# Routing of a two-layer convolution and mixture-of-experts decoder step: the order of the mixer's tail, bf16 one-hot products for the ids, and the place of the first x gather

## The reference

```
h = layer_norm(ALPHA * h + m, ln1_g[i], ln1_b[i])          # m = mixer output
f = hierarchical_moe(h, ...)                               # below
h = layer_norm(ALPHA * h + f, ln2_g[i], ln2_b[i])

def hierarchical_moe(h, ...):
    glog = x @ rg_w + rg_b ; gprob = softmax(glog) ; gp, gidx = top_k(gprob, 1)      # 4 groups
    elog = (x @ re_w + re_b).reshape(-1, 4, 8) ; sel = the chosen group's 8 logits
    ew, eidx = top_k(softmax(sel), 2) ; ew = ew / ew.sum(-1)
    out = sum over the 2 experts: gate * (silu(x @ w_gate) * (x @ w_up)) @ w_down   # 32 experts, width 256
```

## Time and profile before

| | |
|---|---|
| median of 3 runs | 1351.43 us (1350.01 to 1351.71) |
| profiled execution, device time | 1347.05 us |
| its span in the profile | 1345.2 us |
| PE busy | 1036.2 us (77%) |
| DVE busy | 698.4 us (52%) |
| ACT busy | 323.8 us (24%) |
| POOL busy | 288.0 us (21%) |
| DMA | 277.49 MB, mean 206 GB/s |
| mean granted PE clock | 0.889 of full speed |

### The profile page before, as it was taken

The page is one execution under the profiler, slowest core; times in us unless marked ns, Lnnn a source line. Parts: engine busy times, 40 slices in busy tenths (PEclk is TensorE's granted clock), DMA queues, the critical chain, the costliest instruction groups (busy, mean ns, idle before and its releaser), DMA issues.

```text
span 1345.2 us, 16536 instructions
## 1 busy us (share of the span) xinstructions
PE 1036.2 (77%) x5223; PEld 636.4 (47%) x5223; DVE 698.4 (52%) x1286; ACT 323.8 (24%) x428; POOL 288.0 (21%) x399
## 2 busy tenths in 40 slices
PE   5999999947877788832869999359947887899940
PEld 4999984533322223311868998234443322233310
DVE  2323133363444444548399999943363444456438
ACT  2222120004333333412310110050004333344310
POOL 3333320001211111103327646000001211122200
PEclk8999999967998889975889999679967989899975
DMA  9251120085999999950130111000085999998933
GB/s 308 58 153 63 63 96 16 32 346 221 404 419 401 402 404 406 397 195 14 48 125 1 64 43 52 0 12 16 31 338 222 419 403 392 405 348 314 384 118 119
DMA packets 71739, 277.49 MB, mean 206 GB/s; under 512 B 14699, under 2 KB 33183, under 8 KB 45919
## 3 DMA queue, kind: packets, MB, share of 16 engines
q1 hardware_dynamic: 56248, 235.16, 44.9%
q10 hardware_dynamic: 4823, 22.09, 4.5%
q0 software_dynamic: 10624, 19.65, 3.9%
HBM read 268.66 MB, written 27.26 MB: 220 GB/s over the span
## 4 chain that ended last, share of the span: by engine, by line
PE 39%; DMA 24%; DVE 24%; SPq 5%; issue 5%; ACT 2%; POOL 0%; DVEq 0%; ACTq 0%; POOLq 0%; PEldq 0%
DMA ring<-in_moe_w_down_dram 21%; DVE ring L1511 14%; PE ps L890 13%; PE ps L910 10%; PE ps L988 7%; PE ps L1003 2%; SPq L421 2%; DMA ring<-in_sc_w_in_dram 1%; PE ps L922 1%; DVE bn L1192 1%; DVE h L1202 1%; DVE h L1415 1%; PE ps L974 1%; DVE h L1417 1%; SPq L414 1%
## 5 line engine op out<-in xcount | busy, mean ns | idle before, releaser
L988 PE MATMUL ps<-arena 128*64 128x512 f32 x1152 | 280.8, 644 | 62.5 <-DVE arena L1375 60.3
L988 PEld LDWEIGHTS ps<-arena 128*64 128x64 f32 x1152 | 87.4, 148 | 252.6 <-issue 159.3
L1511 DVE SCALAR_TENSOR_TENSOR ring<-arena,cvec,ring 128x528 f32<-128x528 f32 x360 | 189.6, 603 | 0.0
L890 PE MATMUL ps<-hT_hi,w_hi 128*128 128x296 f32 x640 | 145.5, 309 | 33.2 <-POOL w_lo L793 12.5
L1374 DVE COPY arena<-ring 128x1024 f32 x144 | 98.9, 687 | 132.2 <-SPq L487 105.6
L793 POOL TENSOR_TENSOR w_lo<-ring,w_hi 128x512 fp32r<-128x512 f32 x80 | 108.9, 1364 | 204.5 <-ACT w_hi L544 204.5
L910 PE MATMUL ps<-ring 128*128 128x512 f32 (+1 forms) x320 | 141.5, 602 | 11.9 <-ACT ring L736 11.9
L1003 PE MATMUL ps<-arena 128*64 128x512 f32 x576 | 131.5, 598 | 21.2 <-DVE arena L1391 21.2
L890 PE MATMUL ps<-hT_hi,w_lo 128*128 128x296 f32 x640 | 141.2, 302 | 0.0
L890 PE MATMUL ps<-hT_lo,w_hi 128*128 128x296 f32 x640 | 141.2, 302 | 0.0
L890 PEld LDWEIGHTS ps<-hT_hi,w_hi 128*128 128x128 f32 x640 | 105.4, 193 | 40.8 <-issue 30.0
(11 more groups left out here) (206 smaller groups left out, 1077.9 us busy)
## 6 DMA issues: line engine op xcount, KB each, us to landing
ring<-in_moe_w_gate_dram SPq DMA_DIRECT2D x64, 1024.0 KB, 7.7
ring<-in_moe_w_up_dram SPq DMA_DIRECT2D x64, 1024.0 KB, 9.9
ring<-in_moe_w_down_dram SPq DMA_DIRECT2D x64, 1024.0 KB, 13.2
ring<-in_sc_w_in_dram SPq DMA_DIRECT2D x12, 1024.0 KB, 12.0
ring<-in_cf_w_pw_dram SPq DMA_DIRECT2D x4, 1536.0 KB, 14.4
ring<-y_rows_dram ACTq DMA_DIRECT2D x6, 1024.0 KB, 7.1
ring<-in_sc_w_out_dram SPq DMA_DIRECT2D x2, 2048.0 KB, 8.4
x_rows_dram<-h ACTq DMA_DIRECT2D x8, 512.0 KB, 2.6
```

The lines of the kernel that those rows point to most:

```text
L890: last = nc.tensor.matmul(ps[:, pair + a, 0:HALF], w[:, i % 2, kc, :], x[:, k, a * HALF:(a + 1) * HALF], start=(k == 0 and w is w_hi and x ...
L988: ins = nc.tensor.matmul(ps[own, B_GU, :], xT_e[:, k, own], w_gu[:, x, c, i * 2 * F:(i + 1) * 2 * F], start=(k == 0), stop=(k == C - 1))
L1511: ins = nc.vector.scalar_tensor_tensor(out=out, in0=src, scalar=cf_tap(k, j), in1=out, op0=ALU.mult, op1=ALU.add)
```

## The change

Four things change, in both layers, and one is added once.

1. **Order of the mixer's tail.** PE's turn of the loop becomes: first half of project(t), turn of tile t-1, second half of project(t), route(t-1). DVE takes each half's `bn_stats` right after it has added that half, copies the turned tile t-1 between the halves, and reads logits t-1 at the end of the turn. ACT writes tile t-1 to `x_dram` and copies its half of `xT` ahead of the root of tile t.
2. **Ids by bf16 one-hot products.** `r_low` and `r_high` are bf16. An id needs more bits than bf16 has, so it is cut once, ahead of the first tail (`cut_ids`, four small DVE instructions), into a high and a low part; PE makes twenty bf16 products instead of ten in fp32.
3. **Ids ahead of the table.** On DVE the making of `yidx` and `xidx` stands ahead of the count of duos.
4. **First x gather ahead of the table.** POOL's first gather waits for `x_stored` and `ids_ready` only; the wait for `tab_ready` and the register load come after it.

```diff
+        id_parts = sb("id_parts", [P, 2, 2 * NT])
...
-        r_low = work[:, 2048:2048 + 2 * NT * P].rearrange("p (i n) -> p i n", n=P)
-        r_high = work[:, 3584:3584 + 2 * NT * NDUO].rearrange("p (i n) -> p i n", n=NDUO)
+        r_low = nc.alloc_sbuf_tensor_at("r_low", [P, 2 * NT, P], BF16, offset=base + 4 * (ARENA - WORK + 2048))
+        r_high = nc.alloc_sbuf_tensor_at("r_high", [P, 2, 2 * NT, NDUO], BF16, offset=base + 4 * (ARENA - WORK + 2048 + NT * P))
...
 (ACT)
                 for t in range(NT + 1):
-                    if t < NT:
-                        deviation(i * NT + t)
                     if t >= 1:
-                        copy_hT((i + 1) * NT + t - 1)
                         act.wait_ge(ln_done, i * NT + t)
                         n = ROWS[t - 1]
                         act.dma_start(x_dram[(t - 1) * P:(t - 1) * P + n, :], h[0:n, t - 1, :]).then_inc(x_stored, 16)
+                        copy_hT((i + 1) * NT + t - 1)
+                    if t < NT:
+                        deviation(i * NT + t)
...
 (POOL)
-                pool.wait_ge(tab_ready, l + 1)
-                last = last_duo(pool)
...
                 pool.wait_ge(x_stored, 16 * NT * (l + 1))
+                pool.wait_ge(ids_ready, l + 1)
                 load_x(0)
+                pool.wait_ge(tab_ready, l + 1)
+                last = last_duo(pool)
                 pool.wait_ge(x_turned[l], 1)
...
 (PE)
+                def turn(t):
+                    pe.wait_ge(ln_done, NT * 2 * layer + t + 1)
+                    turn_h(NT * (2 * layer + 1) + t)
+
+                for t in range(NT):
+                    if t >= 2:
+                        pe.wait_ge(z_done, 2 * NT * layer + 2 * (t - 1))
+                    project(layer, t, 0)
+                    if t >= 1:
+                        turn(t - 1)
+                    project(layer, t, 1)
                     if t == NT - 1:
                         pe.wait_ge(proj_done, 2 * NT * (layer + 1))
                         pe.sem_inc(mixer_slots_used, 2)
-                    if t >= 2:
-                        route(layer, t - 2)
                     if t >= 1:
-                        pe.wait_ge(ln_done, NT * 2 * layer + t)
-                        turn_h(NT * (2 * layer + 1) + t - 1)
+                        route(layer, t - 1)
+                turn(NT - 1)
                 route(layer, NT - 1)
...
-                    last = nc.tensor.matmul(ps[:, B_IDS, 0:NDUO], r_low[:, i, :], r_high[:, i, :],
-                                            start=(i == 0), stop=(i == 2 * NT - 1))
+                    for part in range(2):
+                        last = nc.tensor.matmul(ps[:, B_IDS, 0:NDUO], r_low[:, i, :], r_high[:, part, i, :],
+                                                start=(i == 0 and part == 0), stop=(i == 2 * NT - 1 and part == 1))
...
 (DVE, the loop of the tail)
+                        nc.vector.tensor_tensor(x, ps[0:n, 2 * (t % 2) + half, :], x, ALU.add).then_inc(z_done, 1)
+                        dve.wait_ge(z_done, i + 1)
+                        ins = nc.vector.bn_stats(bn[0:n, t, half, :], x)
+                        if half == 0 and t >= 1:
+                            turned(t - 1)
+                    step(ins)
+                    aggregate(m)
+                    ln_apply(m)
+                    if t >= 1:
+                        read_logits(layer, t - 1)
+                turned(NT - 1)
+                read_logits(layer, NT - 1)
...
+            def cut_ids():
+
+                dve.wait_ge(iota_made, 9)
+                whole, part = posi[:], posh[:, 0]
+                flat = ids[:].rearrange("p c t -> p (c t)")
+                step(nc.vector.tensor_copy(whole, flat))
+                step(nc.vector.tensor_scalar(part, whole, LOW_IDS, LOW_IDS, ALU.logical_shift_right, ALU.logical_shift_left))
+                step(nc.vector.tensor_copy(id_parts[:, 0], part))
+                step(nc.vector.tensor_tensor(id_parts[:, 1], flat, id_parts[:, 0], ALU.subtract))
...
-                step(tt(r_high, r_high, ids[:].rearrange("p c t -> p (c t)").unsqueeze(2).to_broadcast([P, 2 * NT, NDUO]),
-                        ALU.mult))
...
+                step(tt(r_high[:], r_here.unsqueeze(1).to_broadcast([P, 2, 2 * NT, NDUO]),
+                        id_parts[:].unsqueeze(3).to_broadcast([P, 2, 2 * NT, NDUO]), ALU.mult))
```

More of the change, by code:

```diff
@@ L898, in product_T, with project @@
                 pe.sem_inc(w_used, 1)
-            def project(layer, t):
+            def project(layer, t, half):
                 n = ROWS[t]
                 n0 = SEQ_MIX[layer] + MIX_SLOTS[layer] - 2
-                if t >= 2:
-                    pe.wait_ge(z_done, 2 * NT * layer + 2 * (t - 1))
-                for half in range(2):
-                    w = slot(n0 + half)[:, 0:C * DH].rearrange("p (j n) -> p j n", j=C)
-                    pe.wait_ge(weights_ready, n0 + half + 1)
-                    for j in range(C):
-                        last = nc.tensor.matmul(ps[0:n, 2 * (t % 2) + half, :], mixT[:, j, t * P:t * P + n],
-                                                w[:, j, :], start=(j == 0), stop=(j == C - 1))
-                    last.then_inc(proj_done, 1)
+                w = slot(n0 + half)[:, 0:C * DH].rearrange("p (j n) -> p j n", j=C)
+                pe.wait_ge(weights_ready, n0 + half + 1)
+                for j in range(C):
+                    last = nc.tensor.matmul(ps[0:n, 2 * (t % 2) + half, :], mixT[:, j, t * P:t * P + n],
+                                            w[:, j, :], start=(j == 0), stop=(j == C - 1))
+                last.then_inc(proj_done, 1)
             def route(layer, t):
@@ L926, in mixer_tail @@
             def mixer_tail(layer):
-                for t in range(NT + 1):
-                    if t < NT:
-                        project(layer, t)
+                def turn(t):
[8 more added lines that the diff above has]
+                    project(layer, t, 1)
                     if t == NT - 1:
@@ L1217, in mixer_tail, with turned @@
             def mixer_tail(layer):
-                for t in range(NT + 2):
-                    m = NT * 2 * layer + t
-                    if t < NT:
-                        n = ROWS[t]
-                        dve.wait_ge(h_scaled, NT * 2 * layer + t + 1)
-                        for half in range(2):
-                            i = 2 * NT * layer + 2 * t + half
-                            dve.wait_ge(proj_done, i + 1)
-                            x = h[0:n, t, half * DH:(half + 1) * DH]
-                            nc.vector.tensor_tensor(x, ps[0:n, 2 * (t % 2) + half, :], x, ALU.add).then_inc(z_done, 1)
-                        dve.wait_ge(z_done, 2 * NT * layer + 2 * t + 2)
-                        ln_stats(m)
-                        ln_apply(m)
-                    if t >= 2:
-                        read_logits(layer, t - 2)
-                    if 1 <= t <= NT:
-                        copy_hT(NT * (2 * layer + 1) + t - 1)
+                def turned(t):
+                    copy_hT(NT * (2 * layer + 1) + t)
@@ new lines, in mixer_tail @@
+                for t in range(NT):
+                    m, n = NT * 2 * layer + t, ROWS[t]
+                    dve.wait_ge(h_scaled, NT * 2 * layer + t + 1)
+                    for half in range(2):
+                        i = 2 * NT * layer + 2 * t + half
+                        dve.wait_ge(proj_done, i + 1)
+                        x = h[0:n, t, half * DH:(half + 1) * DH]
+                        nc.vector.tensor_tensor(x, ps[0:n, 2 * (t % 2) + half, :], x, ALU.add).then_inc(z_done, 1)
[4 more added lines that the diff above has]
+                    step(ins)
+                    aggregate(m)
+                    ln_apply(m)
+                    if t >= 1:
+                        read_logits(layer, t - 1)
@@ L1344, in route @@
                     dve.wait_ge(weights_ready, SEQ_MIX[layer] + 2)
+                dve.wait_ge(ids_turned, layer + 1)
+                found = ps[:, B_IDS, 0:NDUO]
+                step(nc.vector.tensor_scalar(idt[:], found, 0.5, blank[:, 0:1], ALU.is_lt, ALU.mult))
+                step(nc.vector.scalar_tensor_tensor(out=yidx[:], in0=found, scalar=-1.0, in1=idt[:], op0=ALU.add, op1=ALU.add))
+                nc.vector.tensor_scalar(xidx[:], yidx[:], 1, None, ALU.logical_shift_right).then_inc(ids_ready, 1)
                 tiles = incl[0:1, 0, E - 1:E]
@@ L1351, in route @@
                     nc.vector.tensor_scalar(tab[:, T_LAST + i:T_LAST + i + 1], duos, float(i + 1), None, ALU.subtract)
-                dve.wait_ge(ids_turned, layer + 1)
-                found = ps[:, B_IDS, 0:NDUO]
-                step(nc.vector.tensor_scalar(idt[:], found, 0.5, blank[:, 0:1], ALU.is_lt, ALU.mult))
-                step(nc.vector.scalar_tensor_tensor(out=yidx[:], in0=found, scalar=-1.0, in1=idt[:], op0=ALU.add, op1=ALU.add))
-                nc.vector.tensor_scalar(xidx[:], yidx[:], 1, None, ALU.logical_shift_right).then_inc(ids_ready, 1)
```

(1 more changed line is left out.)

15 lines of the change are left out of this document (9 added, 6 removed).

## The result

The changed kernel took 1339.21 us at the median of 6 runs (1336.55 to 1346.42), the kernel before 1351.4 (1348.71 to 1351.71): ratio 0.9923, 95% interval 0.9896 to 0.9951. The ratio is estimated from all the runs and is not the quotient of the two medians: it stands for 10.4 us, while the medians lie 12.2 us apart. The forecast of 1343 us is a ratio of 0.9938.

The account below looks back on a forecast made before the run. Bound by a chain of short single steps ahead of the expert loads, no engine or queue full. Tail, ids and table, and gather give 3.9 us in layer 0 and 4.65 in layer 1: 1351.43 - 8.5 = 1343 us, range 1339.5 to 1348.5.

Parts of the forecast that it names:

- The tail: End of the mixer: the reordering starts the last turn 1.05 us earlier in layer 0 and 2.0 in layer 1.
- the rival in which the tail gains nothing: Mixer's tail: half-way turns stall PE or the last turn meets something else; 5.4 us gained, 1346, chance 0.07.
- Ids and table: DVE routing: bf16 id products and ids first remove DVE's waits; table 2.2 us earlier a layer.
- The price of `r_high`: DVE, ids: 500 elements instead of 250 cost 0.26 us more.
- The bound of 4.2 us: PE's id products: upper bound, twenty at a lone one's 0.21 us, leaving things as they were; 0.8 was taken.
- The gather: Expert stage's start: earlier first x gather ends ACT's wait for it; 0.61 us in layer 0, 0.45 in layer 1.
- The first rival: Expert stage's start: gather overlaps expert loads and takes 8.2 us; gain 4.2 us, 1347.2, chance 0.18.
- The sum: Both layers up to the first gate and up product: 3.9 us plus 4.65, together 8.5 us gained.
- what is gained at the start is carried to the end: Behind the first gate and up product nothing changes; copies, loads and stream follow it, so 8.5 us reach the end.
- the rival in which the loads swallow the gain: Expert load stream: its start is set by something that doesn't move, so the gain goes; 1351, chance 0.06.
- the slower case: First gate and up product: PE's clock stays low another 22 us over two layers, costing 11 us; 1354, chance 0.04.
- The range: Whole kernel: 1339.5 us if the clock helps, to 1348.5 with the late gather and 1.3 us of clock.

Follow-up runs that it names:

- `tail_only`: Kernel before with only the new order of the mixer's tail; 1348.36 us against 1349.12, ratio 0.9983.
- `no_gather`: The full change with POOL's first gather put back behind the table; ratio 0.9938 to the kernel before.
- `swap`: The full change with ACT's first copy of the turned rows ahead of its two scalings; 1338.05 us, ratio 0.9916 to the kernel before, in two measurements.
- `swap_warm`: `swap` plus seven PE products a layer whose results are never read, to raise PE's clock; ratios 0.9932 and 0.9917 to the kernel before.
- the second comparison: The unaltered full change measured again beside the kernel before on one chip; 1340.68 us against 1348.58, ratio 0.9943.
- `late`: The full change with 16 more unread DVE instructions ahead of the ids in each layer; 1357.26 us, ratio 1.0066 to the kernel before.

## Why the prediction was right, and where not

**The tail (forecast 1.05 and 2.0 us).** Right in kind: the last turn waits for the norm alone. Against the profile from which it was reckoned, measured 0.94 and 1.6 to 2.0. DVE's last sum to the end of the norm is 278.69 + 1.28 - 275.62 = 4.35 us, for which 4.31 was reckoned, and a start of the tail 0.17 us later in that execution is not the change's. Layer 1 gains more because the route that stood ahead of the turn ran there almost wholly at the low clock (mean 0.66 of full speed in its first 0.7 us, 0.50 behind); the timeline of PE before, layer 1:

```profile
982.79 3.40 PE L922 MATMUL ps<-rw,arena 128*128 128x36 f32 x16 [2.63 <-DVE arena L1179]
```

That layer 0 gains half as much was a trait of the one execution: in three of four profiles of the old order this route took 3.60 us in layer 0 too, and the term is worth 2.1 there. The prediction counted the order of the pieces; that the route also gets out of the low clock, and what this is worth in other executions, was not in the term. No turn stalled a projection, so the rival in which the tail gains nothing is out, by `tail_only`.

**Ids and table (forecast 2.2).** Measured 2.6. The price of `r_high` was right to the digit (0.68 us for 500 elements), that of `r_low` unmoved at 1.49, PE's twenty products 0.71 us against 0.8. The term was mis-sized by the 0.1 us taken off for waking, which does not exist where DVE no longer waits, and by some 0.3 us by which the instructions stand closer together once none of them waits. The bound of 4.2 us for twenty products at the length of a lone one was far too careful: the records overlap, and the rows with 20 products in 0.71 us had said so.

**The gather (forecast 0.61 and 0.45).** Measured between the change and `no_gather` 0.45 and 0.35, with the table already early. Right in kind: of 5 us by which the gather is issued earlier, ACT's queue lets through less than one, and `swap` shows that it was this queue. The first rival, the gather amid the loads, did not happen. The loads did run on to about 306 us as reckoned (stretches of the changed kernel):

```profile
304.00:305.00 1.00, 0.00 (x0) 0.00 (x0) 0.00 (x0) 0.13 (x1) 0.00 (x0) 0.50 0.93 365
305.00:306.00 1.00, 0.00 (x0) 0.00 (x0) 0.80 (x2) 1.00 (x2) 0.00 (x0) 0.50 0.75 275
306.00:307.00 1.00, 0.00 (x0) 0.00 (x0) 1.00 (x2) 1.00 (x2) 0.00 (x0) 0.50 0.22 86
```

But the gather landed 4.50 us after its issue, no later than the 4.57 of before, at 307.34, 1.3 us after them. In the five other profiles of the full change, `swap` and `swap_warm` PE's first turn started 4.1 to 5.1 us after the issue; of the late gather's 8.2 us there is no sign. The rule of the Trainium skill (page "DMA: Bandwidth & Descriptors", section "Queues, rings and completion order") that a DMA engine takes turns between its queues is not contradicted: it says that the gather shares, not for how long, and here there were only some 2 us to share. It says nothing of the 8.2 us, which are the median amid a full stream, and I should not have read the whole of them into it.

**The sum (8.5 us).** The stage starts moved by 0.93 + 3.31 = 4.2 us and by 1.6 + 3.2 = 4.8, 9.0 together, and by 2.1 + 3.3 and 1.9 + 3.2 = 10.5 where the old tail is taken at its usual length; the second comparison gained 7.9 at the medians (7.7 by the ratio), the first 12.2 (10.4). The ids' term was a little too small, the gather's a little too large, and the tail's in layer 0 half its usual size. That 8.5 lies within 1 us of the second comparison is in part luck, since that comparison is good to some 2 us either way. That what is gained at the start is carried to the end was assumed with one sentence and is the step that deserved most doubt. For the table it holds: `late` carries 16.6 of 16.8, and with it the rival in which the loads swallow the gain is out. For the product alone it fails: `swap_warm`.

**The rivals on the clock and the loads.** The clock rose 5 to 6 us into the product in layer 0, as before (the profile of the change), and the length of that product wandered from 8.45 to 10.00 us between two profiles of the same kernel. That is the largest single scatter within the changed stretch, and larger than the gather's whole gain. The prediction's price for the slower case has a slip: 11 us against 8.5 gained leave 2.5 us lost, which is its 1354 but not "more than 2.7". That case did not come.

**The range.** It began at 1339.5, and the first median was 1339.21. The bounds held the clock and the late gather, not the scatter of the load streams, 6.5 us in layer 0 and 5.6 in layer 1 from profile to profile, which moves even a median of six.

## What to carry to other kernels

In a chain of short steps between two engines, ask for each step which wait ends last once the step ahead is gone, and whose queue that is: here a gather moved up by 5 us was worth less than half a microsecond a layer, because two scalings stood ahead of its reader. Small fp32 products, each with a new stationary matrix, were dear here on a PE at the low clock; a split into two bf16 parts doubled their number and took them from 4.46 to 0.71 us. One profile shows one state of the clock: a route of 2.43 us took 3.60 in three other executions, and the move that took it out of the low clock was worth twice what that profile said. Read a gain of under 1% from distances within the execution and from kernels that undo one part, and test with a deliberate delay whether it is carried to the end; a single pair of spans said 3.5 us here where the medians of the runs said 8 to 12.

## What the runs showed of the hardware

- Ten fp32 products of 128 x 128 by 128 x 25 took 4.46 us, and twenty in bf16 0.71 us, both at the low clock.
- The same route (8 fp32 products) took 1.95 us right behind a projection, in both layers of nine profiles, and 2.43 to 3.60 us behind a pause of 2.6 us, in both layers of the four profiles of the old order, depending on when the granted clock fell from 2.4 to 1.2 GHz.
- An engine's first instruction after the table came 2.1 to 2.4 us after the table's last write, in every version (ACT 304.87 and DVE 305.20 after 302.78 in the changed kernel); the load of the number of duos into a register stands between, and how much of the time is its own no run shows. This is as large as any single term of the change, and nothing in it was moved.
- Seven products a layer whose results are not read brought PE to 2.4 GHz ahead of the stage and shortened its first product from 8.4 to 10.0 us to 7.09, and the kernel as a whole by nothing that could be measured.
